# Two transformer layers with mixtures of experts: router on unnormalised sums, token remainders off VectorE, half-row attention scores

## The reference, cut to what matters

```python
x = layernorm(ALPHA * x + h, ln_g[layer, 0], ln_b[layer, 0])
scores = sigmoid(x @ router_w)                    # [256, 32]
sel = scores + router_b
# best group of 8 by the sum of its two best, then the best two in the group
gate = scores[idx] / sum(scores[idx])
for e in range(32):
    y += combine[:, e] * ((silu(x @ w_gate[e]) * (x @ w_up[e])) @ w_down[e])
x = layernorm(ALPHA * x + y, ln_g[layer, 1], ln_b[layer, 1])
```

## Time and profile before

| | us |
|---|---|
| median of three runs | 736.33 |
| the profiled execution | 735.09 |
| its span, first to last instruction | 733.3 |
| PE busy | 688.5 |
| DVE busy | 330.9 |
| ACT busy | 212.5 |
| POOL busy | 133.0 |

### The profile page before, as it was taken

The page is one execution under the profiler, slowest core; times in us unless marked ns, Lnnn a source line. Parts: engine busy times, 40 slices in busy tenths (PEclk is TensorE's granted clock), DMA queues, the critical chain, the costliest instruction groups (busy, mean ns, idle before and its releaser), DMA issues. The chain is left out here.

```text
span 733.3 us, 10061 instructions
## 1 busy us (share of the span) xinstructions
PE 688.5 (94%) x3657; PEld 389.5 (53%) x3657; DVE 330.9 (45%) x674; ACT 212.5 (29%) x418; POOL 133.0 (18%) x145
## 2 busy tenths in 40 slices
PE   7999899879999999999979898987999999999993
PEld 5989788544433334345546797855333434334551
DVE  4756844772342423224253457467243332423326
ACT  4668452412111211111145237241211111111111
POOL 6003010141201001011019570014120101001000
PEclk9999999999999999999999999999999999999998
DMA  9980029847999999999996009374999999999991
GB/s 310 382 333 2 1 100 423 354 191 296 414 421 421 421 422 420 422 422 421 423 416 267 0 9 421 151 306 182 339 422 420 421 420 422 422 422 421 420 413 68
DMA packets 40359, 237.65 MB, mean 324 GB/s; under 512 B 3824, under 2 KB 4256, under 8 KB 15232
## 3 DMA queue, kind: packets, MB, share of 16 engines
q1 hardware_dynamic: 39408, 235.64, 78.8%
q10 hardware_dynamic: 576, 1.05, 0.4%
q0 software_dynamic: 336, 0.44, 0.3%
HBM read 236.06 MB, written 1.05 MB: 323 GB/s over the span
## 5 line engine op out<-in xcount | busy, mean ns | idle before, releaser
L564 PE MATMUL psum<-ring,work 128*64 128x512 f32 (+2 forms) x1296 | 232.4, 509 | 7.1 <-DVE work L1943 7.1
L564 PEld LDWEIGHTS psum<-ring,work 128*64 128x64 f32 (+1 forms) x1296 | 94.6, 139 | 142.1 <-issue 118.0
L564 PE MATMUL psum<-ring,scratch 128*64 128x512 f32 x512 | 116.9, 598 | 3.7 <-ACT scratch L1409 3.7
L1985 DVE TENSOR_TENSOR scratch<-psum,scratch 128x256 f32<-128x256 f32 x32 | 13.6, 425 | 183.8 <-ACT scratch L1405 183.8
L2061 POOL COPY work<-work 128x512 f32 x60 | 39.1, 654 | 314.2 <-PE psum L564 298.1
L1398 ACT ACTIVATE x_T_rounded<-psum,small 128x512 fp32r<-128x512 f32 x64 | 43.8, 687 | 109.7 <-DVE scratch_rounded L1966 77.9
L564 PEld LDWEIGHTS psum<-ring,scratch 128*64 128x64 f32 x512 | 33.9, 136 | 68.8 <-issue 63.6
L1405 ACT ACTIVATE scratch<-psum 128x256 f32<-128x256 f32 x32 | 12.3, 384 | 195.6 <-PE psum L564 195.6
L564 PE MATMUL psum<-ring_rounded 128*128 128x256 f32 (+1 forms) x214 | 66.1, 309 | 0.0
L564 PE MATMUL psum<-ring_rounded,x_T_rounded 128*128 128x512 f32 x192 | 60.9, 398 | 1.0 <-DVE work_rounded L1814 0.9
L564 PE MATMUL psum<-x_T_rounded,scratch_rounded 128*128 128x512 f32 x128 | 56.7, 443 | 0.9 <-issue 0.7
(11 more groups left out here) (253 smaller groups left out, 868.6 us busy)
## 6 DMA issues: line engine op xcount, KB each, us to landing
ring<-in_moe_w_gate SPq DMA_DIRECT2D x64, 1024.0 KB, 15.5
ring<-in_moe_w_up SPq DMA_DIRECT2D x64, 1024.0 KB, 19.6
ring<-in_moe_w_down SPq DMA_DIRECT2D x64, 1024.0 KB, 20.1
ring<-in_diff_w_qkv SPq DMA_DIRECT2D x5, 2048.0 KB, 19.6
ring<-in_diff_w_o SPq DMA_DIRECT2D x1, 4096.0 KB, 14.6
ring<-in_mla_w_o SPq DMA_DIRECT2D x1, 4096.0 KB, 35.9
ring<-in_mla_w_q_b SPq DMA_DIRECT2D x1, 2304.0 KB, 29.5
ring<-in_mla_w_kv_b SPq DMA_DIRECT2D x1, 2048.0 KB, 28.2
```

The source lines that it names most:

```text
L564: return pe.matmul(dst, lhsT, rhs, start=start, stop=stop, skip_group_check=True)
L1985: dve.tensor_tensor(h_sb, psum[:, 6, FF:2 * FF], act_s, ALU.mult).then_inc(m["h_ready"], 1)
```

## The change

Five things are changed together.

- **Scores.** The queries are kept once (`qT`, `qr`), and the score products use 64 rows of the array each, two products on different row halves one after the other. In latent attention two heads are made together, in four banks, ahead of the transposes of heads 1 and 3 only. The zeros and their waits go.
- **Norm and router.** The sums are transposed as soon as they are added, before their mean is known, and copied out plainly. The router's weights are multiplied by the norm's scale beforehand; two row sums (`router_rows`, a product with ones) and the mean and root of each token are put on the logits by VectorE. `router_rows` waits for the router's weights and stands ahead of the adds on VectorE. The normalisation in place comes behind the copy of the logits. The products of zeros in front of the transposes go.
- **Remainders.** `hi` is a plain copy with contiguous reads. `lo` is made by TensorE as ident x tokens - ident x hi, and copied out by ScalarE. Products of zeros behind the router drop from 28 to 6.
- **Offsets.** With VectorE's remainders gone the window offsets follow the one-hots directly.
- **GpSimd.** The diagonals wait for the end of the sort products.

```diff
-MOVED = (2, 3, 4, 6, 7, 8)
+SCORE_BANKS = (0, 1, 6, 7)
+MOVED = (1, 2, 3, 4, 5, 6)
-START_WAIT, FIRST_WAIT, TOP_WAIT, SORT_WAIT = 14, 8, 28, 8
-NORM_WAIT = {1: (8, 4), 2: (11, 0), 3: (8, 4)}
+START_WAIT, FIRST_WAIT, NORM_WAIT, TOP_WAIT, SORT_WAIT = 14, 8, (11, 0), 6, 8
...
                     for c in range(2):
-                        bank = psum[:, 2 * (h % 2) + c, :]
-                        mm(bank[:, 0:3 * P], slope[:, h % 2, :], dist_b[:, :], True, False)
-                        mm(bank[:, 0:P], qz[:, h, c, 0:P], kT[:, h, 0:P], False, False)
-                        mm(bank[:, P:3 * P], qz[:, h, c, P:SEQ], kT[:, h, :], False, True).then_inc(s["sc_ps"], 1)
+                        mm(banks[c][:, 0:3 * P], slope[:, h % 2, :], dist_b[:, :], True, False)
+                    for c in range(2):
+                        mm(banks[c][:, 0:P], qT[rows[c], h, 0:P], kT[rows[c], h, 0:P], False, False)
+                    for c in range(2):
+                        mm(banks[c][:, P:3 * P], qT[rows[c], h, P:SEQ], kT[rows[c], h, :], False, True)\
+                          .then_inc(s["sc_ps"], 1)
...
+                def scores(first):
+                    heads = (first, first + 1)
+                    if first >= 4:
+                        pe.wait_ge(*s("sc_read", first - 2))
+                    for h, bank in zip(heads, banks):
+                        mm(bank[:, 0:P], qnT[:, h, 0:P], knT[:, h, 0:P], True, False)
+                        mm(bank[:, P:3 * P], qnT[:, h, P:SEQ], knT[:, h, :], False, False)
+                    for h, bank, r in zip(heads, banks, rows):
+                        mm(bank[:, 0:P], qr[r, h, 0:P], krT2[r, 0:P], False, False)
+                    for h, bank, r in zip(heads, banks, rows):
+                        mm(bank[:, P:3 * P], qr[r, h, P:SEQ], krT2[r, :], False, True).then_inc(s["sc_ps"], 1)
                 scores(0)
-                scores(1)
                 group(10)
+                scores(2)
                 group(11)
-                scores(2)
...
                 for h in range(HEADS):
-                    if 1 <= h < HEADS - 3:
+                    if h in (1, 3):
                         scores(h + 3)
                     transposes(h)
-                    if h == 0:
-                        scores(3)
...
-                transpose_x(2 * l + 1)
-                pe.wait_ge(ld_rw, 16 * (l + 1))
+                for t in range(TT):
+                    pe.wait_ge(z_ready, TT * l + t + 1)
+                    for half in range(2):
+                        for k in range(4):
+                            last = pe.transpose(psum[:, RAW_BANKS[l][2 * t + half], k * P:(k + 1) * P],
+                                                xs[:, t, 4 * half + k::KD], ident)
+                        last.then_inc(xt[2 * l + 1]["ps"], 1)
+                mm(psum[:, ROW_BANK[l], 0:2 * EXPERTS], ones, routing()["rows"], True, True).then_inc(m["lg_ps"], 1)
+                pe.wait_ge(*xt[2 * l + 1]("sb", KD))
...
-                keep_clock(TOP_WAIT)
+                for t in range(TT):
+                    pe.wait_ge(*ln[2 * l]("norm", (1, 3)[t]))
+                    for c in range(2):
+                        mm(banks[c], ident, xs[:, t, cols[c]], True, False)
+                    pe.wait_ge(*m("hi_ready", t + 1))
+                    for c in range(2):
+                        last = mm(banks[c], minus_ident[:, :], tok_hi[t][:, cols[c]], False, True)
+                    last.then_inc(m["lo_ps"], 1)
+                keep_clock(TOP_WAIT, 0)
...
+                pe.wait_ge(*m("lo_ready", TT))
                 for t in range(TT):
-                    pe.wait_ge(*m("hi_ready", t + 1))
                     pe.wait_ge(*m("hot_ready", t + 1))
-                    pe.wait_ge(*m("lo_ready", t + 1))
...
             def moe(l):
+                root(n, 0)
+                raw_copy(0)
+                root(n, 1)
+                raw_copy(1)
                 act.activation(small[:, 60:61], eps[:, :], ACT.Sigmoid)
-                act.wait_ge(*m("lgt_ps", 1))
+                act.wait_ge(*m("lg_ps", 2))
                 act.copy(logit_T, psum[:, 0, 0:SEQ]).then_inc(m["lgt_sb"], 1)
-                act.wait_ge(*m("lg_ps", 1))
-                act.activation(routing()["score"], psum[:, 1, 0:64], ACT.Sigmoid).then_inc(m["score"], 1)
+                normalise(0)
+                act.wait_ge(*m("logit", TT))
+                act.activation(routing()["score"], routing()["sel"], ACT.Sigmoid).then_inc(m["score"], 1)
+                normalise(1)
...
-                        for c in range(2):
-                            rows = slice(c * DH, (c + 1) * DH)
-                            dve.tensor_scalar(qz[rows, heads_of(g), c, :], src[rows, :, :], DH ** -0.5, None,
-                                              ALU.mult).then_inc(qkv_dve, 1)
+                        dve.tensor_scalar(qT[:, heads_of(g), :], src, DH ** -0.5, None, ALU.mult).then_inc(qkv_dve, 1)
...
+            def router_rows(l):
+                rows = routing()["rows"]
+                dve.wait_ge(ld_rw, 16 * (l + 1))
+                chain(dve.tensor_tensor(rw_scaled, rw, scaled_by(gcol), ALU.mult))
+                chain(dve.tensor_tensor(rw, rw, scaled_by(bcol), ALU.mult))
+                for i, w in enumerate((rw_scaled, rw)):
+                    dve.tensor_reduce(rows[:, i * EXPERTS:(i + 1) * EXPERTS], w.rearrange("p k e -> p e k"), AX.X, ALU.add)
+                if l == 0:
+                    dve.tensor_scalar(minus_ident[:, :], ident, -1.0, None, ALU.mult)
...
-                dve.wait_ge(*m("hi_ready", 2))
-                chain(dve.tensor_tensor(lo_1[0], xs_tiles(1, 0, 4), hi_1[:, 0:4, :], ALU.subtract))
-                dve.tensor_tensor(lo_1[1], xs_tiles(1, 4, KD), hi_1[:, 4:KD, :], ALU.subtract)\
-                   .then_inc(m["lo_ready"], 1)
...
             diff_attention()
-            layer_norm(0, lambda t, c: dve.wait_ge(wo_ps, 2 * t + c + 1))
+            router_rows(0)
+            raw_layer_norm(0, lambda t, c: dve.wait_ge(wo_ps, 2 * t + c + 1))
...
-                pool.tensor_copy(hi_0, xs_tiles(0, 0, KD)).then_inc(m["hi_ready"], 1)
+                pool.tensor_copy(tok_hi[0], xs[:, 0, :]).then_inc(m["hi_ready"], 1)
...
                 pool.wait_ge(*m("key_ready", 1))
+                pool.wait_ge(*m("sort_ps", KD))
```

178 lines of the change are left out of this document (99 added, 79 removed).

## The result

Eleven runs of the changed kernel gave a median of 732.67 us, eleven of the kernel before beside them 738.26; the ratio is 0.9931, 95% interval 0.9915 to 0.9948. In a later session the changed kernel had 732.63 and a ratio of 0.9946 (0.9925 to 0.9967). So the change takes off 0.5 to 0.7%, some 4 to 5 us; 730.0 was predicted, range 725 to 736. The eleven runs of the kernel before lie 1.9 us above the median of three (736.33) from which the forecast was made, so the forecast is better read as a difference: -6.3 us was said. The profiled execution took 732.67 with a span of 730.3, 3.0 us less than the one before.

The account below looks back on a forecast made before the run. TensorE's stream was taken as the bound (busy 688.5 of 733.3 us). Layer 0 attention -4.3, its front -1.0, latent attention +1.2 and layer 1's front -2.45 sum to -6.55; median 729.8, stated as 730.0 us, range 725 to 736.

Parts of the forecast that it names:

- the rival at 733.5: Rival: clock lost in both routers and GpSimd in the way more often; 733.5 us, chance 0.17.
- Scores, -3.2: Layer 0 attention: score products on row halves run side by side, saving 0.40 us a head, 3.2 over eight heads.
- Queries, -1.1: Layer 0 attention: cheaper query writes shorten TensorE's waits behind ScalarE and VectorE by 1.1 us in sum.
- Late add in layer 0, +2.45: Layer 0 router: weights queued behind 8 MB land late, so VectorE's last add starts at 134.65, not 132.20.
- covered, with about 1 us to spare: Router: TensorE's remainders and ScalarE's copies end about 492, before the choice ends at 493.0, so they cost nothing.
- The choice's first instruction: Router: VectorE's first choice instruction stands still beside GpSimd's copy of tile 0, making layer 1's step -1.6, not -2.4.
- The window copies beside the diagonals: After the sort: window copies each wait for up to one GpSimd diagonal, +0.9 us in all (0 to 1.2).
- Front of layer 0, -1.0: Layer 0, router to gate: sort and windows +0.75, gate product keeping its clock -1.7, sum -1.0 (-3.5 to +1.5).
- Latent attention, +1.2: Layer 1 attention: paired heads' scores delay logits, a values group and head 3's transposes; end 1.2 later (0 to +2.0).
- Front of layer 1, -2.45: Layer 1, last add to first gate product: gate at 507.1 in place of 509.56 (-3.3 to -0.5).
- the clock is lost in both routers: Rival: with GpSimd also in the way, layer 1 gives 1.2, layer 0 +1; 733.5 us, chance 0.17.
- Row halves take turns: Slower rival: half-array products not made together, mode changes 0.15 us each, scores +1.2; 738 us, chance 0.08.

Follow-up runs that it names:

- before_rows: Kernel before the change, with only layer 0's score products on 64 rows each, both slope products first; median 736.28 us, ratio 0.9981.
- same_half: Changed kernel with both of a head's score products in layer 0's attention on rows 0 to 63; median 736.83 us, ratio 0.9999.
- after: First profile of the changed kernel, unedited; profiled execution 732.67 us, span 730.3.
- router_early: Changed kernel with layer 0's router weights loaded by GpSimd's own DMA queue in place of SyncE's; median 727.73 us, ratio 0.987.
- halves_in_turn: Changed kernel, layer 0's attention issuing both upper-half score products, then both lower (A0 A1 B0 B1); median 732.73 us, ratio 0.9939.
- latent_spread: Changed kernel, latent attention with both values groups ahead of heads 2 and 3's scores, heads 6 and 7's pair in two parts; median 731.04 us, ratio 0.991.
- the second profile: Changed kernel profiled again without any edit, in a later session; median 732.63 us, ratio 0.9946, span 728.9.
- zeros_back: Changed kernel with products of zeros again in TensorE's router waits from tile 0's transposes to the logit copy; median 730.5 us, ratio 0.9915.
- before: Profile of the kernel before the change, unedited; profiled execution 735.09 us, span 733.3.
- latent_single: Changed kernel, latent attention making scores one head at a time at the former places, each 64-row product alone; median 735.17 us, ratio 0.9978.

## Why the prediction was right, and where not

The time (732.7, and 730.0 was said) lies in the range, and the side was right: the ratio's interval ends at 0.9948. But 732.67 is not below 732.6, the prediction's own mark for faster, and it lies nearer to the rival at 733.5 than to 730.0. Part of that is the level of the runs: as a difference -6.3 us was said and -5.1 (0.69%) measured. The rest is by the prediction's own steps.

- **Scores, -3.2: too much by 1.0.** The step that was mis-sized is the 0.40 us a head; before_rows measured 0.27, or -2.17. Side by side was right, and the factor is the full 2 (same_half). What failed is that the change to half rows had no price in the sum: 0.21 us going in, and the two slope products took 0.43 together in place of 0.32. This leaves 0.33 of the 0.65, and 0.06 more are lost on the way back.
- **Queries, -1.1: right.** 95.80 - 94.5 = 1.3. The wait behind VectorE went, the one behind ScalarE stayed.
- **Missing: the clock in the attention.** 1.5 us in the profiled execution, behind a wait that was already there. Of the eleven profiles here with half-row scores and this wait, four (after, router_early, halves_in_turn, latent_spread) took over 5.7 us from head 4 to head 5, six took 4.3, and same_half 4.9 by its longer scores. The profile of the kernel before had the same wait of 2.33 and no fall. latent_spread lost it a second time, behind an idle 2.34 us ahead of head 0. What decides is open.
- **Late add in layer 0, +2.45: right.** Landing 18.3 us after the issue (18.2 said), the last add 2.37 us later relative to the out-projection (the prediction's own terms add up to 134.55, or 2.35), the clock at 0.50 through the logits in this profile. The choice starts 10.4 us behind the out-projection's end, and 9.7 in the second profile; 8.8 before, and 9.8 by the prediction with its cold logits. That 140.62 on the clock of the span is close to the 140.8 of the prediction is chance, since the attention had moved it by -1.8. router_early proves the cause; the cost is 2 to 4.2 us in the traces, by what the clock does behind the wait.
- **Remainders "covered, with about 1 us to spare": wrong.** The count came late and VectorE's cast waited 0.74 us in layer 0 and 0.60 in layer 1. The term was counted at full clock; with the first identity products at 1.2 GHz the cover is gone (zeros_back brings it back, and in same_half, which kept the clock, it is the count that waits).
- **The sort's products: a term that was put at nothing.** They take 0.4 us more in layer 0 and 0.3 in layer 1.
- **GpSimd.** The choice's first instruction was stretched by 0.13 us in layer 0 and 0.56 in layer 1, 0.8 said. The window copies beside the diagonals were not held up by 0.9 but by 0.1; it was GpSimd that took longer, eight diagonals in 5.81 us in place of 4.67, and the cost came out at the row products (0.43 us of wait). The place was wrong, the sum half of what was said. No run moves the diagonals alone.
- **Front of layer 0, -1.0.** From the out-projection's end to the second gate product: 0.0 in the first profile, -1.0 in the second. The gate product's clock (-1.7) came as said, 5.36 and 5.20 us in before and before_rows behind waits of 3.7, 3.67 in eight of the ten profiles with a wait of 1.95; it fell in zeros_back and latent_spread (5.32 and 5.36).
- **Latent attention, +1.2: right side, 0.7 short.** +1.87: the first logits come 0.8 later (0.7 said), the third 1.4 later as the group behind four heads' scores ends late, and from the seventh on 1.9. latent_spread shows both places.
- **Front of layer 1, -2.45: right in the sum, by parts that cancel.** -2.64 to the first gate product; the 0.5 behind it, at the row products, leaves -2.2 (-2.4 in the second profile). Behind the last add, the first instruction of the choice ended after 6.7 us, where 7.2 was said; the sort ended after 24.8, where 24.3 was said (late count, longer products); the first gate product came 1.9 us behind the sort, where 2.6 was said. The parts of this front, the router on raw sums, the remainders and the offsets, were not run one by one.

In the second profile, which kept its clock in the attention, the four stages give -3.6 - 1.0 + 1.9 - 2.4 = -5.1, where -6.55 was said; the comparison of the runs gives 5.1 us too. The misses that carry the difference are the scores (1.0) and the latent attention (0.7). The first profile's own -3.0 comes out of other pieces and is in part luck: -2.0, 0.0, +1.9 and -2.2 in the four stages, -0.85 between them that is no work of the change, and +0.2 at the start.

Of the rivals, "the clock is lost in both routers" was half true: the clock fell in layer 0 in four of six profiles, and in layer 1 in four of seven, at 134 and at 486 in after. But layer 1 kept its gain, since the fall costs 0.4 to 0.6 us there, on work that was nearly covered. (By the rival's own terms its time is 733.0, not 733.5.) "Row halves take turns" is refuted by same_half.

## What to carry to other kernels

When a step gets a new wait for a load, look at what stands ahead of that load in its queue, and not only at when its data were needed before; a small load goes on a queue of its own. Two products on different row halves cost one, but the change to them and back costs some 0.3 us, so in this kernel they paid in pairs and lost alone. Count work that is said to be covered at the slower clock if TensorE idles ahead of it. And take more than one profile of each kernel before a difference of a microsecond or two is given a cause: here 1.7 of the 3.0 us between two profiles were such a fall of the clock.

## What the runs showed of the hardware that was not expected

- Products on different row halves overlap whether they are issued A0 B0 A1 B1 or A0 A1 B0 B1 (0.86 us either way; 1.51 on the same half).
- A change between full-array and half-row products costs 0.1 to 0.2 us. The Trainium skill (TensorEngine Tiling (Array Packing), Key Properties) says that a change of mode drains the array; the trace agrees that it costs time, by 0.21 us in same_half and 1.99 against 1.30 us a head in latent_single.
- A small load beside 8 MB of others landed in 6.1 us from GpSimd's queue and in 18.3 behind them in SyncE's.
- One and the same kernel, with the same wait of 2.2 us on TensorE, came out of it at 1.2 GHz in one execution and at 2.4 GHz in another (5.74 and 4.27 us for the same work). It also fell behind waits of 2.1, 1.95 and 1.55 us in some profiles and not in others.
- VectorE's small instruction with two SBUF operands ended just behind GpSimd's cast in both layers (140.98 against 140.91, 486.01 against 485.94), while beside GpSimd's diagonals it was these that stretched, from 0.58 to 0.73 us each.
- Weight loads of 128x128 (fp32r) that read with a stride of 8 elements took 0.33 us, contiguous ones 0.19, and the products of the sort followed each other by 0.245 us in place of 0.232.
